# An empty slot behind every second linear attention step in blocks 1 and 2 of a hybrid decoder layer

## The reference, cut to what matters

```
proj = h @ w_in
out_a = rg_lru(xa, ...) * gelu(ya)
out_b = forgetting_attention(fq, fk, fv, ff, ...)
out_c = gated_linear_attention(gq, gk, gv, glow, gg, ...)
mix = concatenate([out_a, out_b, out_c]) @ w_out
x = x + gate1 * mix
gt, up = split(h @ ffn_w_gate_up, 2)
x = x + gate2 * ((silu(gt) * up) @ ffn_w_down)
```

## Time and profile before

| | us |
|---|---|
| median of 3 runs | 2975.97 |
| lowest, highest | 2973.37, 2981.22 |
| the profiled execution | 2978.72 |
| its span, first to last instruction | 2976.9 |

### The profile page before, as it was taken

How to read it: one execution, slowest core, us unless ns; L and a number is a source line. 1 busy time by engine, 2 the same in 40 slices (tenths; PEclk the granted TensorE clock), 3 DMA queues, 4 the chain that set the end, 5 groups by cost and what they waited for, 6 DMA issues and landing times.

```text
span 2976.9 us, 32965 instructions
## 1 busy us (share of the span) xinstructions
PE 2813.1 (94%) x12416; PEld 2209.3 (74%) x12416; DVE 1464.6 (49%) x1876; ACT 1185.6 (40%) x1654; POOL 1036.4 (35%) x488
## 2 busy tenths in 40 slices
PE   8998998888989999999999999999999999999999
PEld 4786876566757787886777777867777777778887
DVE  3968786566554334445443454464445654521111
ACT  3333333343345354444433535454335455332222
POOL 2544454221324332233433222434331122444443
PEclk9999999889989999999999999999999999999999
DMA  7555545626643344444624444445244544423222
GB/s 268 181 157 190 152 140 155 184 82 171 212 130 126 121 122 138 127 152 138 185 82 127 144 139 138 148 149 179 70 142 139 155 147 124 141 92 99 93 99 92
DMA packets 159902, 419.05 MB, mean 141 GB/s; under 512 B 18284, under 2 KB 20604, under 8 KB 156672
## 3 DMA queue, kind: packets, MB, share of 16 engines
q1 hardware_dynamic: 157408, 412.48, 44.2%
q10 hardware_dynamic: 2336, 4.46, 0.4%
HBM read 355.95 MB, written 60.92 MB: 140 GB/s over the span
## 4 chain that ended last, share of the span: by engine, by line
PE 65%; DVE 6%; ACT 3%; issue 3%; DMA 2%; SPq 2%; POOL 1%; ACTq 0%; POOLq 0%; DVEq 0%
PE ff_acc_ps L77 17%; PE ff_acc_ps L78 17%; PE ff_acc_ps L79 17%; PE fa_st_ps L1691 1%; PE fa_s_ps L1665 1%; PE fa_o_ps L1707 1%; PE fa_st_ps L1692 1%; PE fa_s_ps L1666 1%; PE fa_o_ps L1709 1%; PE fa_o_ps L1708 1%; DVE fa_inv_sum L1408 1%; PE fa_st_ps L1744 1%; DVE ff_silu L1371 1%; PE fa_o_ps L1781 1%; SPq L956 1%
## 5 line engine op out<-in xcount | busy, mean ns | idle before, releaser
L1093 POOL TENSOR_TENSOR w_lo<-ff_w_raw,w_hi 128x1024 fp32r<-128x1024 f32 (+1 forms) x326 | 772.6, 2370 | 1614.6 <-PE ff_acc_ps L79 1537.6
L77 PE MATMUL ff_acc_ps<-h_odd_hi,w_hi 128*128 128x512 f32 x1856 | 750.2, 404 | 47.8 <-DVE h_odd_lo L1376 13.3
L78 PE MATMUL ff_acc_ps<-h_odd_lo,w_hi 128*128 128x512 f32 x1856 | 737.4, 397 | 0.0
L79 PE MATMUL ff_acc_ps<-h_odd_hi,w_lo 128*128 128x512 f32 x1856 | 735.9, 396 | 0.0
L1108 ACT ACTIVATE w_hi<-ff_w_raw 128x1024 fp32r<-128x1024 f32 (+1 forms) x326 | 338.8, 1039 | 928.7 <-PE ff_acc_ps L79 714.6
L77 PEld LDWEIGHTS ff_acc_ps<-h_odd_hi,w_hi 128*128 128x128 f32 x1856 | 356.8, 192 | 155.5 <-issue 62.5
L79 PEld LDWEIGHTS ff_acc_ps<-h_odd_hi,w_lo 128*128 128x128 f32 x1856 | 356.4, 192 | 78.0
L78 PEld LDWEIGHTS ff_acc_ps<-h_odd_lo,w_hi 128*128 128x128 f32 x1856 | 357.0, 192 | 72.8 <-issue 1.7
L1401 DVE TENSOR_TENSOR fa_p_lo<-fa_probs,fa_p_hi 128x512 fp32r<-128x512 f32 x240 | 154.4, 644 | 286.8 <-ACT fa_p_hi L1142 286.5
L77 PE MATMUL ff_acc_ps<-ff_a_hi,w_hi 128*128 128x512 f32 x704 | 285.2, 405 | 10.1 <-issue 6.1
L78 PE MATMUL ff_acc_ps<-ff_a_lo,w_hi 128*128 128x512 f32 x704 | 280.1, 398 | 0.0
(11 more groups left out here) (263 smaller groups left out, 4044.1 us busy)
## 6 DMA issues: line engine op xcount, KB each, us to landing
ff_w_raw<-in_w_gate_up SPq DMA_DIRECT2D x176, 512.0 KB, 4.0
w_raw<-in_w_in SPq DMA_DIRECT2D x74, 512.0 KB, 4.2
ff_w_raw<-in_w_down SPq DMA_DIRECT2D x64, 512.0 KB, 3.6
mod_w<-in_w_mod SPq DMA_DIRECT2D x24, 1024.0 KB, 5.3
fa_v<-v_split_dram SPq DMA_DIRECT2D x60, 384.0 KB
ff_w_raw<-in_w_out SPq DMA_DIRECT2D x32, 512.0 KB, 3.9
fa_ks_a<-ka_dram SPq DMA_DIRECT2D x60, 256.0 KB
fa_kt_a<-ka_dram SPq DMA_DIRECT2D x60, 256.0 KB
```

The lines of the kernel that those rows point to most:

```text
L77: nc.tensor.matmul(out, hi, act_hi, start=first, stop=False)
L78: nc.tensor.matmul(out, hi, act_lo, start=False, stop=False)
L79: return nc.tensor.matmul(out, lo, act_hi, start=False, stop=last)
L1093: nc.gpsimd.tensor_tensor(w_lo[:, j % LO, wide], w_raw[:, j % RAW, wide], w_hi[:, j % HI, wide].bitcast(F32), ALU.subtract).then_inc(lo_re ...
```

## The change

```
@@ -676,9 +676,10 @@
         lo += X_STEPS + 1
         g_load.append(lo)
         lo += G_LEAD - 1
+
         for x, (j, s) in enumerate(G_ORDER):
-            side[lo + x] = [[("G", (b, j, s))]]
-        lo += GLA_T * G_STEPS + 1
+            side[lo + (x if b == LAST else x + x // 2)] = [[("G", (b, j, s))]]
+        lo += GLA_T * G_STEPS + 1 + (0 if b == LAST else GLA_T * G_STEPS // 2)
         a_load.append(lo)
         fill_at.append(lo)
         q_fill.append(lo)
```

## The result

| | median, us | lowest, highest | runs |
|---|---|---|---|
| before | 2975.48 | 2970.98, 2983.87 | 18 |
| after | 2985.58 | 2979.51, 2992.3 | 18 |

After takes 1.0028 of before, 95% interval 1.002 to 1.0037. By the ratio the change costs 8.3 us (the two medians stand 10.1 apart), where the prediction gave it a gain of 3. The profiled execution of after took 2983.24 us, its span is 2981.5. Against the 2976.9 of before that is 4.6 us more, and block 1 alone has 11.3 more. The difference is no gain of the change: 5.5 us of it lie ahead of block 1's linear slots, which begin at 898.9 in after and at 904.4 in before. No edit of this document touches anything ahead of them, and in the fourteen profiled executions they begin between 898.9 and 907.4.

The account below looks back on a forecast made before the run. The prediction took TensorE, busy for 94% of the span, as the bound. Its terms summed to -3.2 us: 2978.72 profiled gives 2975.5, and with the median 2.75 lower, about 2973, range 2965 to 2983.

Parts of the forecast that it names:

- the first head slots of block 1: Start of block 1's heads, now gate and up slots with rushed loads: +1.0 us, unit 64's silu in time within 1 us.
- block 1 pays block 2's price: Rival: unit 66's weights land after slot 65, block 1's head start pays 7.5 us for 1.1, 6.4 more: 2978; chance 0.15.
- the parity: Argument against that price: block 1's loads stand in an up slot, first turn in a gate slot, the other way round.
- S and T: Waits for maxima and exponentials in the heads, scaled by turns: +0.4 us in block 1, +1.3 in block 2.
- linear steps, block 2: Pair of s=2 moves to slots 123 and 124; the 3.05 us wait and its clock price go: -4.8 us.
- linear steps, block 1: Pair moves to slots 44 and 45, still adjacent; the 3.11 us wait and 1.7 us of clock stay: 0.
- first M of block 2: M, now behind slot 146's first product, waits 3.2 to 3.3 us for m_cols, plus 1.7 of clock: +5.0 us.
- other M, block 1: Waits for m_cols in block 1's heads, each given a like old place's wait: 2.3 for 3.6 us, -1.3.
- other M, block 2: Waits for m_cols of block 2's last five M, by like old places: 0.9 for 4.7 us, -3.8.
- first head slots, block 2: Start of block 2's heads: one weight load fewer in the rush, 2 us, less 1.0 for a late silu: -1.0.
- The slower rival: Exponentials late in every dense head slot behind a gate in blocks 1 and 2: +14 us, 2990; chance 0.1.
- the three signs that the prediction named for being wrong: Block 1's linear wait goes too (-5 more), M's wait is absent, or waits per head turn exceed 0.1 us.

Follow-up runs that it names:

- e8: After, with block 1's heads one slot earlier and block 2's one slot later, so each starts in the other kind of slot: 3012.58 us, 1.0122 of before.
- e11: Before, with two empty slots among the linear steps of block 2 alone, its heads three turns in each slot: 2967.69 us, 0.9965 of before.
- e12: After, with block 2's heads ending one slot earlier, in 22 slots of four turns in place of 23: 3006.95 us, 1.0088 of before.
- e1: Before, with the change made in block 1 alone: 2988.07 us, 1.0034 of before.
- e3: After, with SyncE issuing the weights ahead of the head loads in the slots of those loads, blocks 1 to 3: 2977.25 us, 0.9998 of before.
- e4: After, with ScalarE's silu or a_hi put ahead of the weight copy in the first head slot of blocks 1 to 3: 2974.19 us, 0.9983 of before.
- e9: After, with the edits of both e4 and e5: 2969.54 us, 0.9968 of before.
- e5: After, with one finish turn of block 1 moved from behind the first to behind the fifth turn of its head: 2982.78 us, 1.0015 of before.
- e10: e9, with block 2's first M one turn later, behind the third product of slot 146: 2967.76 us, 0.9962 of before.
- e6: Before, with the move of e4 (ScalarE's own work ahead of the weight copy in first head slots): 2975.47 us, 0.9997 of before.

## Why the prediction was wrong, step by step

**The step that failed: the first head slots of block 1, "+1.0".** They measured +10.0 (11.1 lost for 1.1). The prediction saw that the loads would rush there, that the slots were now gate and up "the other way round", and that the silu of unit 64 would be in time. That is right: there is no silu wait. It stopped there, at the one path that block 2 had shown. In a slot behind an up the own work of ScalarE is `a_hi`, behind it VectorE's `a_lo`, and behind that the maxima, without which the third score piece has no bank. Every link was in its own description ("what waits within a step holds up all that is behind it on that engine"), and the link from `a_hi` to `a_lo` stands in the earlier trace rows. The count was made for one consumer of the late engine in place of all. The rival with the right place ("block 1 pays block 2's price", 6.4 us more) had the nearest size, by another mechanism (weights that land too late for a silu), and a chance of 0.15 only, against it "the parity". e8 shows that the parity chooses the victim, not whether there is one.

**The step that was mis-sized: S and T, "+0.4 and +1.3".** They were scaled by a rate per turn, 0.067 to 0.072 us in three blocks. Slot 83 alone lost 4.9 us (2.7 of wait and the clock), and block 2's maxima and exponentials came to 5.2 + 0.4 = 5.6 for the 2.9 predicted. The rate isn't one: all waits of S, T and M per head turn are 0.035 us in e11 (3.0 turns in a slot), 0.11 in block 2 of after (3.8) and 0.24 in e12 (4.0). What decides is who stands behind whom: F in a slot's first turn ahead of maxima, M in a slot's first turn. For M the prediction looked at each place, and was right. For F it did not. (The two failed steps and M's waits in block 1, 2.1 us less, make 10.0 + 4.9 - 2.1 = 12.8, where the block has 11.3 more: some 1.5 us of small gains aren't traced.)

The rest of the sum held:

| step | predicted | measured |
|---|---|---|
| linear steps, block 2 | -4.8 | -4.8 (slots 123, 124: 15.9 to 11.1 us) |
| linear steps, block 1 | 0; wait of 3.11 and clock 0.76 stay | 3.11 stays, before slot 46, clock 0.76 |
| first M of block 2 | 3.2 to 3.3 of wait, +5.0 | 3.00 of wait, 4.97 lost |
| other M, block 1 | 2.3 left | 1.5 left |
| other M, block 2 | 0.9 left | 0.7 left |
| late silu of unit 140 | 1.0 | 1.22 |
| silu wait at block 2's heads | about 3 | 2.3 |
| first head slots, block 2 | -1.0 | -1.7 (7.5 to 5.8 lost, slots 141 to 144, with the late silu of unit 140) |

A part of this is luck. The waits of M and of the silu before slot 46 follow from the order of the work and come back in every run that keeps it. The 1.7 us of clock in the price of M do not: the wait of 3.0 us in slot 146 left the clock at 0.87 in four profiled executions, at 0.77 in three and at 1.00 in one.

Of block 2 as a whole I had -3.3, and -0.5 came. The S and T term explains 2.7 of the difference, the first head slots and M take 0.9 back, and about 1.0 us is left that lies in no wait over 0.15 us. It has no experiment of its own and stays open.

The slower rival (exponentials late in dense slots behind a gate, 2990) was right in sign and wrong in mechanism: T waits 0.4 us in all in the heads of blocks 1 and 2 of after. Of the three signs that the prediction named for being wrong, one came: the waits of S, T and M per head turn rose above 0.1 us, to 12.1/60 = 0.20 in block 1 and 9.3/88 = 0.11 in block 2. It says that something waits, not what. The silu wait that was to be "below 1.5 in block 1" was absent and said nothing.

## What to carry over

When work moves to other slots, list for each engine all that stands behind the instruction that will be late, follow every one of them to the engine that waits for it, and do so for the new kind of slot. A path that was harmless in the old slot has left no wait in the trace to be found. Where a late transfer can't be avoided, put what is ready ahead of what waits for it on the engine's queue, and cover the slots behind it too. A rate per item taken from dense stretches isn't a price: check by place where the long instructions (here a reciprocal of 3.36 us) and the dependent ones fall, above all where the count per slot divides the period of the work, since a bad place (e12) or a good one (e11) then comes back with every head.

## What the runs showed of the hardware

**The same wait doesn't always cost the clock.** Nine profiled executions have the wait of 3.1 us before slot 46, in the same surroundings. In six (after, e1, e3, e4, e9, e12) the granted clock behind it is 0.76 and the unit takes 7.1 to 7.2 us, in three (e5, e8, e10) it is 1.00 and the unit takes 5.5 to 5.6. The 1.78 us in slot 143 left 1.00 in before and in e1, and 0.87 in e6. The 3.0 us in slot 146 left 0.77 to 1.00, as said above. In e12 three waits of 2.18 us left 0.88 in block 2, one of 2.18 in block 3 left 1.00. The prediction's rule, 2.18 spares it and 3.11 doesn't, was two samples of this. By the Trainium skill, "TensorE: Matmul & The Clock Gate", section on HAM oscillation, an idle stretch that is long enough throttles TensorE. The traces agree that waits bring it, and also show that the length of the wait alone doesn't tell. What else decides isn't shown by any run here.

**A small VectorE instruction stands still for a GpSimd one.** The cast into `m_cols` takes 0.17 us in slot 146 and 1.64 in some others. The timeline of e12 in slot 149 (its first row GpSimd's split of the weights):

```profile
1697.28 2.36 POOL L1094 TENSOR_TENSOR w_lo<-ff_w_raw,w_hi 128x1024 fp32r<-128x1024 f32 x1 [10.01 <-PE ff_acc_ps L79]
...
1698.03 1.64 DVE L1394 CAST fa_m_cols<-fa_neg_max 128x4 fp32r<-128x4 f32 x1
...
1700.02 0.44 PE L1676 MATMUL fa_s_ps<-fa_ident_r,fa_m_cols 128*68 128x128 f32 x4 [2.18 <-DVE fa_m_cols L1396]
```

The split ends at 1699.64, the cast at 1699.67, and the wait of 2.18 us for M has 1.5 us of it. `a_lo` does the same, with 0.69 us in slot 64, where GpSimd is idle, and 1.67 in e4's, where it isn't. The Trainium skill, "SBUF — State Buffer", section "SBUF: two separate sides", says that VectorE and GpSimd share a pair of ports, and that whichever starts first, a GpSimd instruction or a VectorE one that is in a two-port mode or reads two inputs in SBUF, gets the pair for the whole instruction while the other is blocked. The trace agrees in that the cast ends 0.03 us behind the split, and `a_lo` has two such inputs. Not every small instruction is held: the row reduction just ahead of the cast, at 1697.84 under the same split, takes 0.15 us. Whether the cast, with one input, runs in a two-port mode no run shows. So a part of some of M's waits comes from GpSimd's split at the head of the slot, and no run here tried to move it. In block 2 of after all six casts take 0.17 us; there only the `a_lo` ahead of M in slot 146, with 1.35 us, is longer than alone.
